# One attention step waits a job longer, the later ones follow, and the top-k rounds are dealt out anew

## The reference, cut to what matters

```
for l in range(2):
    h = rms_norm(x, norm_g[l])
    a_u, a_v, a_z, b_q, b_k, b_v, b_z, i_q, i_k, i_w, g_a, g_b = split(h @ w_in[l])
    # branch A: spatial gating
    v = layer_norm(gelu(a_v));  mixed = masked_ws @ v + bs
    y_a = gelu(a_u) * mixed * silu(a_z)
    # branch B: an indexer picks 128 keys for each query, all heads attend to them
    score = sum_h i_w[h] * relu(rope(i_q)[h] @ rope(i_k)) * scale      # chunk-causal
    keep  = top_k(score, 128)
    y_b = softmax(q @ k on keep) @ v * silu(b_z)                       # 4 heads of 128
    merged = sigmoid(g_a + b0) * (y_a @ w_oa) + sigmoid(g_b + b1) * (y_b @ w_ob)
    x = x + merged @ w_out
```

## Time and profile before

| what | value |
|---|---|
| median of 3 runs | 789.74 us (789.71 to 791.07) |
| the profiled execution | 789.07 us, of which the span of the trace is 786.9 us |
| TensorE (PE) busy | 776.5 us, 99% of the span |
| weight loads (PEld) busy | 667.6 us, 85% |
| VectorE (DVE) busy | 617.9 us, 79% |
| ScalarE (ACT) busy | 393.2 us, 50% |
| GpSimd (POOL) busy | 152.0 us, 19% |
| TensorE's waits | 2.2, 1.8, 1.5 and 1.5 us, in four groups |
| granted TensorE clock | 0.998 of full speed over the span |

### The profile page before, as it was taken

One profiled execution on the slowest core, in us unless ns is written; L12 is line 12 of the kernel. 1 busy time (PEld: TensorE's weight loads), 2 busy tenths in 40 slices (PEclk: granted clock), 3 DMA queues, 4 the chain that ended last, 5 costly groups with the idle time before them and its releaser, 6 DMA issues.

```text
span 786.9 us, 11503 instructions
## 1 busy us (share of the span) xinstructions
PE 776.5 (99%) x4124; PEld 667.6 (85%) x4124; DVE 617.9 (79%) x1058; ACT 393.2 (50%) x718; POOL 152.0 (19%) x137
## 2 busy tenths in 40 slices
PE   7999999999999999999999999999999999999998
PEld 7988888888788889988899888888887888899886
DVE  5779999979767667769986799999786666656895
ACT  6576656341354336745564765543324434467242
POOL 1257511100010103012211674110000101120130
PEclk9999999999999999999999999999999999999999
DMA  9634238733264237785873532478222723397684
GB/s 333 221 120 123 79 107 167 155 107 107 80 161 96 67 80 114 201 260 111 193 234 108 166 84 73 134 155 194 76 85 87 181 82 55 79 160 257 146 145 124
DMA packets 51561, 108.38 MB, mean 138 GB/s; under 512 B 3376, under 2 KB 8688, under 8 KB 51504
## 3 DMA queue, kind: packets, MB, share of 16 engines
q0 software_dynamic: 18896, 39.93, 26.7%
q1 hardware_dynamic: 32320, 67.12, 26.6%
q10 hardware_dynamic: 288, 0.59, 0.2%
HBM read 90.85 MB, written 6.29 MB: 123 GB/s over the span
## 4 chain that ended last, share of the span: by engine, by line
PE 87%; DVE 10%; issue 1%; DMA 1%; ACT 1%; DVEq 0%; SPq 0%; ACTq 0%
PE bank L836 17%; PE bank L838 17%; PE bank L837 17%; PE bank L957 6%; PE bank L903 3%; PE bank L905 3%; PE bank L904 3%; PE bank L873 3%; PE bank L875 3%; PE bank L874 3%; PE bank L810 2%; PE bank L828 2%; DVE w_lo L1403 2%; PE bank L766 1%; PE bank L819 1%; PE bank L781 1%
## 5 line engine op out<-in xcount | busy, mean ns | idle before, releaser
L1403 DVE TENSOR_TENSOR w_lo<-w_raw,w_hi 128x1024 fp32r<-128x1024 f32 x144 | 186.5, 1310 | 11.2 <-ACT w_hi L1042 6.7
L1042 ACT ACTIVATE w_hi<-w_raw 128x1024 fp32r<-128x1024 f32 x144 | 148.2, 1054 | 21.4 <-DMA w_raw<-in_w_out 14.7
L836 PE MATMUL bank<-h_lo,w_hi 128*128 128x512 f32 x320 | 128.0, 400 | 0.0
L838 PE MATMUL bank<-h_hi,w_hi 128*128 128x512 f32 x320 | 124.8, 390 | 0.0
L837 PE MATMUL bank<-h_hi,w_lo 128*128 128x512 f32 x320 | 124.5, 389 | 0.0
L836 PE MATMUL bank<-w_lo,h_hi 128*128 128x512 f32 x256 | 100.5, 392 | 0.0
L838 PE MATMUL bank<-w_hi,h_hi 128*128 128x512 f32 x256 | 99.9, 390 | 0.0
L837 PE MATMUL bank<-w_hi,h_lo 128*128 128x512 f32 x256 | 99.8, 390 | 0.0
L838 PEld LDWEIGHTS bank<-h_hi,w_hi 128*128 128x128 f32 x320 | 60.0, 188 | 12.9
L836 PEld LDWEIGHTS bank<-h_lo,w_hi 128*128 128x128 f32 x320 | 60.1, 188 | 12.3
L837 PEld LDWEIGHTS bank<-h_hi,w_lo 128*128 128x128 f32 x320 | 60.1, 188 | 12.2
(11 more groups left out here) (206 smaller groups left out, 1731.7 us busy)
## 6 DMA issues: line engine op xcount, KB each, us to landing
w_raw<-in_w_in SPq DMA_DIRECT2D x92, 512.0 KB, 4.2
w_raw<-in_w_in POOLq DMA_DIRECT2D x16, 512.0 KB, 6.0
w_raw<-in_w_out POOLq DMA_DIRECT2D x16, 512.0 KB, 6.3
w_raw<-in_w_out SPq DMA_DIRECT2D x12, 512.0 KB, 4.2
out<-x_sb POOLq DMA_DIRECT2D x4, 1024.0 KB, 6.1
w_raw<-in_w_oa SPq DMA_DIRECT2D x8, 512.0 KB, 4.2
w_raw<-in_w_ob SPq DMA_DIRECT2D x8, 512.0 KB, 3.6
x_sb<-out POOLq DMA_DIRECT2D x2, 2048.0 KB, 10.9
```

The lines of the kernel that those rows point to most:

```text
L836: nc.tensor.matmul(dst, s_h, m_l, start=(n == 0), stop=False)
L838: last = nc.tensor.matmul(dst, s_h, m_h, start=False, stop=(n == len(pairs) - 1))
L1042: nc.scalar.activation(hi, w_raw[:, raw_slot(layer, u)], ACT.Copy).then_inc(s_whi.sem, 1)
L1403: nc.vector.tensor_tensor(lo, w_raw[:, raw_slot(layer, u)], hi.bitcast(F32), ALU.subtract) \
```

## The change

```diff
-_slots = list(range(JOB_ZA[2], JOB_GA[-1] + 1)) + JOB_OA[1::2] + JOB_GB[0:7:2]
+_slots = JOB_ZA[2:3] + JOB_GA + JOB_OA[1::2] + JOB_GB[0:9:2]
-SPLIT_YB = {JOB_GB[8]: [0, 1], JOB_GB[9]: [2], JOB_GB[10]: [3]}
+SPLIT_YB = {JOB_GB[9]: [0, 1], JOB_GB[10]: [2], JOB_GB[11]: [3]}
 TOPK_SLOTS = {10: [(1, 1)], 11: [(1, 1)], ...
-              23: [(2, 1), (3, 2)], 26: [(3, 1)], 28: [(3, 2)], 29: [(3, 1)], **{s: [(3, 2 if s in (34, 36) else 1)] for s in range(32, 40)}}
+              23: [(2, 1), (3, 1)], 24: [(3, 1)], 25: [(3, 1)], 33: [(3, 1)], 34: [(3, 1)], 35: [(3, 1)], 36: [(3, 2)],
+              37: [(3, 1)], 38: [(3, 1)], 39: [(3, 2)], 40: [(3, 1)], 42: [(3, 1)], 44: [(3, 1)], 46: [(3, 1)]}
```

## The result

The changed kernel takes 794.32 us (median of 6 runs, 793.49 to 796.62) against 789.75 us (788.79 to 791.07, 6 runs) of the kernel before on the same chip. The ratio is 1.006, with a 95% interval of 1.0045 to 1.0075: slower by 4.6 us. The forecast was 791.6 us and its range ended at 793.2, so the direction came as forecast and the time lies outside the range. The profiled execution took 794.11 us with a span of 792.0 us, 5.1 us more than the span before.

The account below looks back on a forecast made before the run. TensorE was taken as the bound (87% of the chain), standing only where it waits for VectorE. Old waits -2.08 and new stalls +3.90 gave +1.82 us on 789.74, so 791.6 us, range 788.6 to 793.2.

Parts of the forecast that it names:

- What goes, -2.08: Behind `za3`: TensorE's waits for VectorE's scaling, 0.86 and 1.22 us, vanish once the step moves behind `ga0`; -2.08 us.
- Ahead of the attention, 0: Rounds added at `zb0` and `zb1`: the layer norm still ends 1.3 us before TensorE wants it; costs nothing, 1.5 at most.
- The `oa` jobs, the mechanism: Rounds put into `oa` jobs and `ga7` overfill VectorE's queue, so TensorE waits for the scaling behind `gb0` in both layers.
- The `oa` jobs, the size: VectorE's 34.60 us against TensorE's 32.65: 1.95 us late behind `gb0` per layer, +3.90 us; upper bound 2.6 per layer.
- Weighing the rule: VectorE's evacuations: 0.24 us gaps counted by the trace row, against the skill's rule that semaphores after instructions cost nothing extra.
- Two stalls: Rival: the remainder in `gb5` also misses `gb6`, 0.5 to 1 us more per layer, 792.6 to 793.6 us; chance 0.08.

Follow-up runs that it names:

- e1: Changed kernel with the top-k rounds back in their old places, so only the attention steps move; 786.85 us, ratio 0.9965 to the kernel before.
- f4: Kernel before, steps unmoved; rounds of `zb2`, `za0`, `za1` and one of `u3` moved to `zb0`, `zb1` and `ga`; 788.06 us, ratio 0.9985.
- e2: Changed kernel with the four `oa` rounds and one of two in `ga7` moved to `ga0` to `ga5`; 788.55 us, ratio 0.9984 to the kernel before.
- e3: Changed kernel plus nine unused matmuls in front of the transposes behind `gb0`, in both layers; 792.19 us, ratio 1.0031 to the kernel before.
- e4: Changed kernel with the round of `oa4` moved to `ga1`; 789.54 us, ratio 0.9995 to the kernel before.
- f1: Changed kernel run again unaltered, for a second trace; 793.55 us, ratio 1.0058 to the kernel before.
- f2: Changed kernel plus nine unused matmuls in front of the transposes behind `gb0`, in layer 0 alone; 791.54 us, ratio 1.0036 to the kernel before.
- f3: Changed kernel with the round of `ga1` moved to `oa1`, one more in the second part; 798.05 us, ratio 1.0104 to the kernel before.

## Why the prediction was wrong

- **What goes, -2.08: the mechanism right, the size open.** No wait at `za3` or `ga0`. Both halves of the change take it away alone (`e1`, `f4`). `e1` is 1.7 to 3.9 us faster than before, `f4` 0.5 to 1.8 and `e2` 0.6 to 2.0.
- **Ahead of the attention, 0: right.** No wait of TensorE between start-up and the `oa` jobs in the trace after. (The kernel before had one short wait more behind 12 us than the prediction says, 0.20 us at 24.66; it changes nothing.)
- **The `oa` jobs, the mechanism: right.** Wait behind `gb0`, for the scaling, in both layers, no idle time of VectorE for TensorE before it. Taking a round out and putting one in moved the stalls by 1.49 and 1.40 us where the sum has 1.51.
- **The `oa` jobs, the size: too small.** The prediction had "eight evacuations, 266.67 to 267.61 = 0.94 each". That row is an evacuation ahead of a weight remainder. Four of the eight stand ahead of a maximum and take 1.03 to 1.05 us, the others 0.91 to 0.93. In layer 1 this makes 7.82 us instead of 7.52. Another 0.10 us is the start: step 8's maximum begins 0.95 us behind its scores (648.36 to 649.31) instead of 0.85. Together that is the 0.4 us between 2.35 and 1.95. In layer 0 the evacuation ahead of step 11 takes 1.38 us, another 0.35, and the stall is 2.71. This longer one stands at the same place in the traces of `e3`, `e4`, `f1`, `f2` and `f3`, and never in layer 1. In `e1` it is another job's, ahead of a remainder, so it doesn't come from step 11's maximum; what makes it isn't shown. The row that would have shown a part of this was in view, 268.75 to 269.79 = 1.04; its bracket named TensorE, and I took the tenth of a microsecond as TensorE's. Term: +5.06 instead of +3.90, and 2.71 is also beyond the 2.6 that I gave as its bound.
- **The step that was missing: the clock.** The prediction ended with "late by 1.95 us ... TensorE stands for this time", as if a stall cost its own length. Behind 2.71 us it cost 1.57 more. `e3` shows it, with the same stall and no drop, and `f3` has the drop in layer 1 too, where the last stall is now 2.72 us; so it isn't bound to the layer. No term and no rival had it, though the trace of the kernel before holds a drop, in start-up. It alone is larger than the error of the size, and without it the time would be 794.32 - 1.57 = 792.75 us, inside the range.
- **Weighing the rule: the row was right.** The gaps of 0.24 us behind evacuations are in VectorE's queue again, of 0.35 us ahead of a maximum, and they are part of what TensorE waited for. By the section The DRAIN you can't avoid (the Trainium skill, VectorE: DVE Perf Modes) they would not have cost anything. The rule speaks of a chain of copies; here the next instruction waits for the evacuation's own end, and the trace shows that wait.
- **Two stalls: did not come.** With 0.4 us of margin the remainder in `gb5` met `gb6` without a wait.

The new sum, by the rows of after: -2.08 + 5.06 + 1.57 = +4.55, against 4.57 us between the medians. The agreement is luck in part: the runs scatter by over 1 us, and the terms come from one execution with a mean clock of 0.998, while the five others have 0.996 or 0.997.

## What to carry to other kernels

When a step is moved to a place where its partner is late, price every wait for an instruction's own end by the pair of instructions that will stand there, not by one pair for all. A stall of TensorE has a second price, the clock behind it, and it comes in a jump: look in the kernel's own traces for stalls of that length with full clock behind them, and where there are none, let the range reach over the drop. A wait that can't be taken away was cheaper here with idle matmuls in it. Before that, look for idle time of the late engine just ahead of the stretch: `e2` moved the rounds forward, and the wait was gone.

## What was new about the chip

- In the attention stretch the drop isn't proportional to the stall. Stalls of 2.71 and 2.72 us (2.54 us idle in the rows) had a drop behind them four times of four: twice in the changed kernel, twice in `f3`. Stalls of 2.35 us had none in three, and those of 1.22 us and less none. Each drop cost 1.34 to 1.58 us. The length of one stall isn't the whole of it: in start-up the kernel before has a drop behind two waits of only 1.47 and 1.33 us idle (before 9.34 and 11.74 us), and `f4` has none behind 1.27 and 1.26 at the same place. What else counts, the moment of the stall or the work around it, isn't settled by these cases.
- What a drop in start-up costs isn't shown. The kernel before has one in its trace (mean granted clock 0.53 from 13.0 to 15.6 us), at a place where the DMAs are busy all the time (DMA share 1.08). Of its 24 runs in the first batch, ten had a mean clock of 0.997 to 0.999 and a median of 789.78 us, fourteen one of 1.000 and a median of 790.12. In the second batch it is the other way round: six under 1.000 have a median of 789.82 us, eleven at 1.000 one of 788.99.
- A part of the scatter between runs comes at the layer's end. In the traced execution of `e1`, the slowest of its six, ScalarE waited 2.37 us for a weight piece, and the layer norm behind it was late:

```profile
386.51 1.06 ACT L1042 ACTIVATE w_hi<-w_raw 128x1024 fp32r<-128x1024 f32 x1 [2.37 <-DMA w_raw<-in_w_out]
```

```profile
392.01 1.09 PE L751 MATMUL bank<-eye,xn 128*128 128x128 f32 x8 [0.57 <-DVE xn L1699]
393.74 0.50 PE L873 MATMUL bank<-w_lo,h_hi 128*128 128x512 f32 x1 [0.64 <-DVE x_sb L1634]
```

  In `f4`'s trace, the slowest of its eleven, ScalarE waited 2.54 us there and TensorE 0.64; in `e2`'s ScalarE waited 1.67 us and TensorE not at all. A single traced span is therefore uncertain by over a microsecond, and a comparison has to go by the same stretch in both traces, or by medians of many runs.
